# An eleventh place in the weight ring, one norm step for both tiles, and expert loops written out

## The reference

```
def reference(x, ...):
    h = x
    h = h + token_mixer(rmsnorm(h, norm_mix_w), w_in, ..., w_branch, w_out)
    h = h + moe_ffn(rmsnorm(h, norm_ffn_w), w_router, b_router, w_mlp1, b_mlp1, w_mlp2, b_mlp2)
    return rmsnorm(h, norm_final_w)

def moe_ffn(xn, ...):                       # 32 experts, top 4 of them for each token
    ...
    hdn = xb @ w_mlp1[e] + b_mlp1[e]        # 1024 -> 2048
    glu = minimum(hdn[:, :1024], 7); lin = clip(hdn[:, 1024:], -7, 7)
    act = glu * sigmoid(1.702 * glu) * (lin + 1)
    y   = act @ w_mlp2[e] + b_mlp2[e]       # 1024 -> 1024
    ...                                     # weighted sum over a token's four experts
```

## Time and profile before

| what | us |
|---|---|
| median of 3 runs (1125.34 to 1125.79) | 1125.36 |
| the profiled execution | 1125.41 |
| its span, first to last instruction | 1123.6 |
| PE busy (share of the span) | 1085.1 (97%) |
| VectorE busy | 367.8 (33%) |
| ScalarE busy | 245.6 (22%) |

### The profile page before, as it was taken

The page is one execution under the profiler, slowest core; times in us unless marked ns, Lnnn a source line. Parts: engine busy times, 40 slices in busy tenths (PEclk is TensorE's granted clock), DMA queues, the critical chain, the costliest instruction groups (busy, mean ns, idle before and its releaser), DMA issues.

```text
span 1123.6 us, 14458 instructions
## 1 busy us (share of the span) xinstructions
PE 1085.1 (97%) x5409; PEld 487.5 (43%) x5410; DVE 367.8 (33%) x813; ACT 245.6 (22%) x345; POOL 3.6 (0%) x12
## 2 busy tenths in 40 slices
PE   9999999999999999999999999999999999999996
PEld 8888888533333333333333333333333333333332
DVE  5977787422222222222222222222222222212223
ACT  4845674311111111111111111111111111111112
POOL 0000000000000000000000000000000000000000
PEclk9999999999999999999999999999999999999999
DMA  9655469999999999999999999999999999999996
GB/s 336 223 157 165 155 204 417 428 420 416 428 427 436 430 430 429 432 428 433 435 432 395 429 433 435 433 432 432 430 429 430 433 435 432 432 432 430 426 423 253
DMA packets 37877, 439.15 MB, mean 391 GB/s; under 512 B 5244, under 2 KB 5432, under 8 KB 21880
## 3 DMA queue, kind: packets, MB, share of 16 engines
q1 hardware_dynamic: 37488, 437.78, 93.3%
q10 hardware_dynamic: 360, 0.95, 0.3%
HBM read 437.67 MB, written 1.05 MB: 390 GB/s over the span
## 4 chain that ended last, share of the span: by engine, by line
PE 79%; DMA 14%; DVE 6%; issue 0%; ACT 0%; SPq 0%; DVEq 0%; PEldq 0%; ACTq 0%
PE bank L1154 33%; PE bank L1181 18%; DMA ring<-in_w_mlp_dram 11%; PE bank L798 9%; DMA late_slots<-in_w_mlp_dram 4%; PE bank L1083 3%; PE bank L1165 2%; PE bank L792 2%; PE bank L963 2%; PE bank L1011 2%; DVE xn L1670 2%; DVE xn L1667 2%; DVE xn L1674 2%; PE bank L1059 1%; PE bank L1067 1%; PE bank L1133 1%
## 5 line engine op out<-in xcount | busy, mean ns | idle before, releaser
L1154 PE MATMUL bank<-ring,xn 128*64 128x512 f32 x1232 | 276.3, 595 | 6.3 <-DMA ring<-in_w_mlp_dram 6.3
L1154 PE MATMUL bank<-late_slots,xn 128*64 128x512 f32 x880 | 197.5, 596 | 4.9 <-DMA late_slots<-in_w_mlp_dram 4.9
L1154 PEld LDWEIGHTS bank<-ring,xn 128*64 128x64 f32 x1232 | 84.4, 136 | 163.8 <-issue 150.3
L1181 PE MATMUL bank<-ring,smo 128*64 128x512 f32 x624 | 138.3, 595 | 0.0
L705 ACT ACTIVATE xn<-bank 128x512 f32<-128x512 f32 x33 | 19.7, 598 | 481.5 <-PE bank L1154 481.5
L1154 PEld LDWEIGHTS bank<-late_slots,xn 128*64 128x64 f32 x880 | 60.2, 136 | 117.9 <-issue 106.3
L1683 DVE SCALAR_TENSOR_TENSOR moe_y_lo<-bank,st,moe_y_hi 128x512 fp32r<-128x512 f32 x33 | 24.8, 750 | 235.5 <-ACT moe_y_hi L712 235.5
L1667 DVE TENSOR_SCALAR xn<-bank 128x512 f32<-128x512 f32 x33 | 22.8, 691 | 220.9 <-PE bank L1154 220.9
L1181 PE MATMUL bank<-late_slots,smo 128*64 128x512 f32 x416 | 92.1, 595 | 0.0
L1181 PEld LDWEIGHTS bank<-ring,smo 128*64 128x64 f32 x624 | 42.9, 137 | 81.1 <-issue 81.1
L712 ACT ACTIVATE moe_y_hi<-bank,st 128x512 fp32r<-128x512 f32 x33 | 22.7, 687 | 233.7 <-PE bank L1181 233.7
(11 more groups left out here) (270 smaller groups left out, 890.9 us busy)
## 6 DMA issues: line engine op xcount, KB each, us to landing
ring<-in_w_mlp_dram SPq DMA_DIRECT2D x43, 4096.0 KB, 30.4
late_slots<-in_w_mlp_dram SPq DMA_DIRECT2D x29, 4096.0 KB, 28.0
ring<-in_w_mlp_dram SPq DMA_DIRECT2D x28, 2048.0 KB, 13.4
late_slots<-in_w_mlp_dram SPq DMA_DIRECT2D x15, 2048.0 KB, 15.6
ring<-in_w_in_dram SPq DMA_DIRECT2D x22, 1024.0 KB, 5.4
late_slots<-in_w_mlp_dram SPq DMA_DIRECT2D x8, 1024.0 KB, 38.5
ring<-in_w_branch_dram SPq DMA_DIRECT2D x4, 1024.0 KB, 5.0
ring<-in_w_out_dram SPq DMA_DIRECT2D x4, 1024.0 KB, 7.1
```

Source lines behind the costliest of these rows:

```text
L1154: last = mm(B[4 + u][g * C:(g + 1) * C, :], xgT[:, k % 4, k // 4, :], by_group(held[k // 2][0][:, k % 2, u * FF:(u + 1) * FF], g), start=F ...
L1181: last = mm(B[7][g * C:(g + 1) * C, :], actT[:, j, h * C:(h + 1) * C], held[4 + h][0][:, j // 2, (j % 2) * D + g * N:(j % 2) * D + (g + 1) ...
```

## The change

- The ring has eleven places in all; `once` is gone, chunk m always goes to place m % 11, and it waits for chunk m - 11. Before, that held for chunks 11 to 15, and chunks from 16 on waited for chunk m - 10.
- 58 pairs of chunks go as one DMA of 4 MB, where 72 did: a pair that is not adjacent in SBUF (m % 11 of 3 or 9) goes as two.
- The first loads use the same semaphores and the same number of chunks behind each, with other chunk numbers.
- On PE and SP the loop over rounds is written out: every expert has its own code, with constant counts to wait for. `scatter_b2` stands ahead of expert 16.
- Of the last four chunks, the two odd ones (chunks 3 and 5 of expert 31) are cut in three pieces: 1 MB, 0.5 MB, 0.5 MB.
- The first norm: mean, root and reciprocal once for both tiles; tile 1's product on ScalarE; 12 fillers in place of 14.
- The final norm: the mean of tile 1 comes between the two halves of tile 0, and its reciprocal behind them.

```diff
-PLACES = 10
-ROUND = PLACES // 2
-QUADS = range(ROUND + 1, E - 2)
+FIRST_QUADS = 6
+PLACES = 11
+QUADS = [m for m in range(CHUNKS * FIRST_QUADS, CHUNKS * (E - 2), 2) if m % PLACES not in (3, PLACES - 2)]
...
                 if pieces == 2:
-                    for half, done in enumerate((place_landed[place], piece_landed[i])):
-                        sp.dma_start(places[place][:, half, :], src[:, half * SLOT:(half + 1) * SLOT]).then_inc(done, 16)
-                elif place is None:
-                    sp.dma_start(once[:, :, :].rearrange("p a n -> p (a n)"), src).then_inc(once_landed, 16)
+                    at = [0, SLOT, 2 * SLOT] if i % 2 == 0 else [0, SLOT, SLOT + FF, 2 * SLOT]
+                    for a, b, done in zip(at, at[1:], (place_landed[place], piece_landed[i], half_landed.get(i))):
+                        sp.dma_start(places[place].rearrange("p a n -> p (a n)")[:, a:b], src[:, a:b]).then_inc(done, 16)
...
+            for e in range(E - 1):
+                after = sp.value_load(first_item[0:1, e + 1:e + 2], min_val=1, max_val=ITEMS - 1)
+                for i in range(CHUNKS):
+                    m = CHUNKS * e + i + PLACES
+                    if m >= CHUNKS * E:
+                        continue
+                    if m not in QUADS and m - 1 not in QUADS:
                         wait_freed(after, i)
-                        load(e - c + (m + PLACES) // CHUNKS, (m + PLACES) % CHUNKS, (m - 1) % PLACES, pieces(m + PLACES))
-                    elif i % 2:
+                        load(m // CHUNKS, m % CHUNKS, m % PLACES, 2 if m >= CHUNKS * (E - 1) + 2 else 1)
+                    elif m - 1 in QUADS:
                         wait_freed(after, i)
-                        load_quad(e + 1 if i == 1 else e + 2, (i // 2 + 2) % 3, (m - 2) % PLACES)
...
             act.wait_ge(s_x, 16 * TT)
             nc.scalar.activation(xn[:, 1, :], xs[:, 1, :], ACT.Square, accum_out=st[:, 1:2]).then_inc(sumsq, 1)
             norm_root()
+            act.wait_ge(rstd, TT)
+            nc.scalar.activation(xn[:, 1, :], xs[:, 1, :], ACT.Copy, scale=st[:, 7:8]).then_inc(xn_ready, 1)
...
-            keep_warm(14, hm[:, :, :, :].rearrange("p t h d -> p (t h d)"))
+            keep_warm(12, hm[:, :, :, :].rearrange("p t h d -> p (t h d)"))
...
                     for u in range(2):
+                        if u and k == KB - 1 and 3 in in_halves:
+                            pe.wait_ge(*in_halves[3])
...
+                        if j == 3 and 4 + h in in_halves:
+                            pe.wait_ge(*in_halves[4 + h])
...
-            experts(0, chunks)
-            pe.wait_ge(opened, 2 * TT)
-            scatter_b2()
-            with pe.Fori(1, (E - 2) // ROUND) as r:
-                experts(r, lambda c: chunks_in_round(c, r))
+            for e in range(1, E - 1):
+                if e == E // 2:
+                    pe.wait_ge(opened, 2 * TT)
+                    scatter_b2()
+                first = after
+                after = pe.value_load(first_item[0:1, e + 1:e + 2], min_val=1, max_val=ITEMS - 1)
+                with pe.Fori(first, after) as i:
+                    item(i, chunks(e))
...
-            for t in range(TT):
-                norm(t)
-                v.tensor_scalar(xn[:, t, :], xs[:, t, :], st[:, 6 + t:7 + t], None, ALU.mult).then_inc(xn_ready, 1)
+            v.tensor_scalar(st[:, 2:2 + TT], st[:, 0:TT], 1.0 / D, EPS, ALU.mult, ALU.add).then_inc(meansq, TT)
+            dve.wait_ge(root, TT)
+            v.reciprocal(st[:, 6:6 + TT], st[:, 4:4 + TT]).then_inc(rstd, TT)
+            dve.wait_ge(rstd, TT)
+            v.tensor_scalar(xn[:, 0, :], xs[:, 0, :], st[:, 6:7], None, ALU.mult).then_inc(xn_ready, 1)
...
-            final_scale(0)
+            final_rstd(0)
+            final_half(0, 0)
             final_mean(1)
-            final_scale(1)
+            final_half(0, 1)
+            final_rstd(1)
+            final_half(1, 0)
+            final_half(1, 1)
```

More of the change, by code:

```diff
@@ L115, in landings @@
     for m in range(CHUNKS * E):
[L116 to L121, removed]
+        place = m % PLACES
+        if m - 1 in QUADS:
             table.append(table[-1])
@@ L200, in build @@
         pair = [ring[:, at:at + 2, :] for at in range(0, RING, 2)]
[L201 to L206, removed]
+        late_pair = [late[:, 2 * i:2 * i + 2, :] for i in range(5)]
+        places = late_pair[1:5] + pair + late_pair[0:1]
+        quads = {n: late[:, at:at + 4, :] for n, at in ((PLACES - 1, 0), (0, 2), (1, 4), (2, 6))}
+        quads.update({4 + n: ring[:, 2 * n:2 * n + 4, :] for n in range(5)})
+        assert sgm_at == sga_at + 4 * SLOT and sga_at + 4 * 2 * SLOT >= late_at + 4 * 10 * SLOT
+        wfin = places[(CHUNKS * (E - 2) + 2) % PLACES][:, 0, 0:D]
         wgh = nc.alloc_sbuf_tensor_at("w_gate_hi", [P, KB, P], F32R, offset=sgm_at)
@@ L418, in _ @@
             sp.wait_ge(slots_used, Q_OUT + 2)
-            load(1, 0, 5)
-            load(1, 2, 7)
+            first_load(1)
+            first_load(6)
             sp.wait_ge(slots_used, Q_MOE)
-            load(1, 1, 6)
-            load(1, 3, 8)
-            load(1, 4, 9)
+            first_load(2)
+            first_load(7)
+            first_load(10)
             sp.wait_ge(firsts, 1)
[L427 to L439, removed]
-                for i in range(chunks):
-                    m = CHUNKS * c + i
-                    if not (whole_second if i < 2 else whole):
+            for e in range(E - 1):
[5 more added lines that the diff above has]
+                    if m not in QUADS and m - 1 not in QUADS:
@@ L451, in _ @@
[L451 to L456 removed]
+                        load_quad(m // CHUNKS, m % CHUNKS // 2, (m - 1) % PLACES)
             after = sp.value_load(first_item[0:1, E - 1:E], min_val=1, max_val=ITEMS - 1)
[L458 removed]
+            wait_freed(after, 3)
@@ L1219, in _ @@
             v = nc.vector
-            def norm(t):
-                n = t + 1
-                dve.wait_ge(sumsq, TT)
-                v.tensor_scalar(st[:, 2 + t:3 + t], st[:, t:t + 1], 1.0 / D, EPS, ALU.mult, ALU.add).then_inc(meansq, 1)
-                dve.wait_ge(root, n)
-                v.reciprocal(st[:, 6 + t:7 + t], st[:, 4 + t:5 + t]).then_inc(rstd, 1)
-                dve.wait_ge(rstd, n)
             v.memset(hm[:, 0, 0:2, :], 0.0).then_inc(zeros, 1)
@@ L1696, in final_scale, with final_half @@
                 dve.wait_ge(rstd, 2 * TT + t + 1)
-                for n in range(2):
-                    cut = slice(n * N, (n + 1) * N)
-                    v.scalar_tensor_tensor(out=xn[:, t, cut], in0=B[2 * t + n][:, :], scalar=st[:, 6 + t:7 + t],
-                                           in1=wfin[:, cut], op0=ALU.mult, op1=ALU.mult).then_inc(normed, 1)
+            def final_half(t, n):
+                cut = slice(n * N, (n + 1) * N)
+                v.scalar_tensor_tensor(out=xn[:, t, cut], in0=B[2 * t + n][:, :], scalar=st[:, 6 + t:7 + t],
+                                       in1=wfin[:, cut], op0=ALU.mult, op1=ALU.mult).then_inc(normed, 1)
             dve.wait_ge(s_small2, 16)
```

88 lines of the change are left out of this document (32 added, 56 removed).

## The result

| | median us | runs | ratio to before, 95% interval |
|---|---|---|---|
| before | 1125.36 (1124.67 to 1128.31) | 11 | |
| the changed kernel | 1127.54 (1126.02 to 1131.29) | 11 | 1.0026 [1.0016, 1.0037] |

The change makes the kernel slower by 0.26%, 2.9 us of 1125.4. The forecast was 1124.1 with a range up to 1127.3, so the result lies outside it and on the other side. The profiled execution took 1127.33 us (span 1125.5), 1.92 more than that of before. *Written out* means that a loop's body stands in the program once for each pass.

A forecast was written before the change was run, and what follows sets the result against it. PE was taken to bound the mixer, DMA everything from about 170 us on. Terms -0.9 - 1.2 + 1.1 + 0.9 - 0.95 - 0.3 = -1.35 on the profiled 1125.41 us gave 1124.1, range 1121.3 to 1127.3.

The forecast's parts named there:

- Code written out: PE's loop copies: 22 more instruction packets cost +3.3 us, less 2.4 for two late landings avoided; sum +0.9, ends -2.4 and +24.
- the half at the end: Part of the -2.4: before's landing at 1100.97 took 60.1 us where 58.7 was due; the change should avoid this.
- The half at 275 us: Part of the -2.4: a packet on level engines made a landing 1.2 us late; the change should avoid this.
- Rival A: Instruction packets hide, spread over all 16 engines or falling into gaps: 1122.2 us, or 1120.7 with no cost; 23%.
- Rival B: Packets hit few engines, nothing levels them, lag adds up: sum +2.0 us with four engines, +8.6 with two; 10%.
- Eleventh place: In the ring: chunks from 16 on issued one chunk earlier, filling the rate dip at 240 to 260 us; -1.2 us.
- Last expert: At the end: 0.5 MB pieces let half of eight records run before chunk 3's last piece lands; -0.95 us.
- final norm: At the tail: tile 1's mean behind one half, so its root comes earlier and the last halves start sooner; -0.3 us.
- First norm: At the start: two fewer fillers and earlier norm let PE's first product start at 11.6 instead of 12.48; -0.9 us.
- Fewer pairs: In the weight stream: 14 pairs go as 28 slightly slower DMAs of 2 MB, plus the third pieces; +1.1 us.
- `scatter_b2`, 0: On PE: the same work moved to a place where PE has lead costs nothing; 2 us if the lead were gone.

The follow-up runs named there:

- written-out kernel: The kernel before with only the loops over rounds on PE and SP written out; 1128.95 us, ratio 1.0029.
- all but the place: The kernel before with everything of the change except the eleventh place in the ring (ten places, 72 DMAs of 4 MB); 1128.44 us, ratio 1.0019.
- norm and tail: The kernel before with the new first norm, third pieces and new final norm order, loops and ten places as before; 1123.1 us, ratio 0.9981.
- filler products: The changed kernel with two unused products on PE ahead of the waits for chunks 0 and 2 of experts 24 to 29; 1127.63 us, again 1127.47.
- smaller late DMAs: The changed kernel with all chunks of experts 27 to 31 in DMAs of 2 MB or less; 1127.1 us, ratio 1.0015.
- three rounds written: The kernel before with experts 16 to 30 written out on PE only, SP as before; 1130.28 us, ratio 1.0043, 5 runs.
- tail alone: The kernel before with only the last expert's third pieces and the new order of the final norm; 1124.2 us, ratio 0.9985.
- fillers and late pairs: The changed kernel with both the unused products on PE and no DMA of 4 MB from expert 27 on; 1128.53 us, ratio 1.0024.

## Why the prediction was wrong

- **Code written out, +0.9: the step that failed.** The prediction took 22/8 x 1.2 = +3.3 for the packets and set -2.4 against it, because before "paid for a packet on level engines twice where after should not". Alone, the edit costs +3.3 [+2.1, +4.4]. That this is the forecast's first half is luck, since both halves were off. The packets cost more: the landings lose 4.0 us to 17 packets in the written-out kernel, 2.9 to 16 in all but the place, 0.18 to 0.24 a packet where 0.15 was taken. Of the -2.4, the half at the end came (1.4 of slack for 1.2): at the landing of 1100.97 before's last engine went from 0.5 to 1.6 us behind the mean, and in the written-out kernel that landing brought nothing new. The half at 275 us had been read from one execution: from the eleventh chunk's landing to that of chunks 66 and 67, norm and tail gained 1.1 on before with before's loops, the written-out kernel 1.2. The rotation over eight engines is borne out, by the table above and by the durations of the packets, which repeat with period eight from 629.9 us on (1.087, 1.018, 1.018, 1.074, 1.069, 1.060, 1.099, 1.099 us, then 1.086, 1.018, 1.018, 1.073, 1.069 ...).
- **Rival A** (packets hide) is refuted. The rule of the Trainium skill ("Runtime: NRT & Kernel Launch", section "Instruction fetch mechanics") that the crossing of a block is mostly hidden holds here for PE: the item stays 26.77 us. It does not hold for the DMA engines that carry 430 GB/s of weights beside it.
- **Rival B** named what happens to the engines: with eleven places nothing levels them at 600 us, and the lag of the first 500 us is kept. It was given 10%, with engines hit four or two at a time; it was eight in turn. As a price it is not borne out: behind 613 us lag adds up with ten places too, and the landings lose as much there.
- **Eleventh place, -1.2.** The dip at 240 to 260 went as read, and chunks 66 and 67 landed 2.45 us earlier (503.98 for 506.43); 0.7 of it is the start, and norm and tail, with ten places, had them 1.36 earlier. At chunk 89 1.16 were left. "The landing was not late, so nothing is won there" was right for 600 us. Against the kernel without the place nothing is left (1.0026 against 1.0019).
- **TensorE's clock** was in no term. The prediction read PE's waits only as slack, and asked neither how long PE would stand nor what the clock does then: 1.5 us in the chain, 1.1 to 1.4 by the ratios, with the doubt told above.
- **Last expert, -0.95, and final norm, -0.3.** Alone they give -1.7 [-2.7, -0.7], so size and sign stand. In the changed kernel the piece gave nothing, because the end was by then bound by PE from the landing of chunks 176 and 177 on. The prediction did not ask how far behind that bound stood: 1.4 us.
- **First norm, -0.9.** In the trace -0.82 at the first product; by the runs -0.7, not told from 0, but 1.5 to 1.7 group against group. In the changed kernel PE waits 0.23 for ScalarE, which the prediction had covered with 0.4: the product took 1.15, not 1.06, and started later.
- **Fewer pairs, +1.1.** 430 instead of 432 GB/s from 640 to 980 us fits: 340 x 2/432 = 1.6 for pairs and packets, of which 13 packets of 1.1 us over 16 engines are 0.9. It was not tried alone. **`scatter_b2`, 0:** it shows in no wait.
- **What adds up.** Written out +3.3, norm and tail -2.1 make +1.2 for the kernel without the place; measured +2.1 [1.1, 3.2]. The sum lies inside, at the edge.

In the changed kernel's own profile, 1.92 over that of before, the terms come out like this, by landings:

| term | forecast | profile |
|---|---|---|
| start, at the landing of the eleventh chunk | -0.9 | -0.7 |
| eleventh place, and the late packet at 275 us (to chunk 67) | -1.2 - 1.2 | -1.75 |
| packets and fewer pairs (chunk 67 to 177) | +3.3 + 1.1 | +4.8 |
| end: late packet and last pieces | -1.2 - 0.95 | -1.4 |
| TensorE's clock | none | +1.5 |
| final norm | -0.3 | -0.5 |
| sum | -1.35 | +1.95 |

So in this one execution the largest miss is the clock, and the others are 0.2 to 0.8 each. The two terms at the end draw on one wait of 1.4 us and could not both be had.

Left open: the price of the clock in a typical run, and why the filler products and the smaller late DMAs together (1.0024) gave no more than either (1.0014 to 1.0017, and 1.0015); the intervals overlap, and the profile of the two together started late.

## What to carry to other kernels

Where DMA is the bound, a landing goes by the slowest of the 16 engines. Compare landings and the MB moved at them, not the rate alone: a stream can be ahead in its sum and late in its landings, as this one was by 1.3 and 2.4 us. A dip of the rate is worth filling only if the slowest engine idles in it. Code that is fetched while weights stream was paid for on those engines here, though the engine that runs it never waited; keep the loop. And before crediting a shorter wait at the end, work out where the next bound stands behind it, and how long PE will stand elsewhere.

## What the runs showed of the hardware

- An instruction packet of 16 KB held one DMA engine 1.02 to 1.10 us, and PE's packets went to eight of the sixteen engines in turn; one packet for each of the eight went with a landing 1.4 us later. PE ran 26.8 us of items on one such packet without waiting, and the loop over five experts ran with none at all from 500 to 1090 us.
- PE's granted clock fell to 1.2 GHz for 3.41 us behind waits of 2.29 to 3.30 us in the middle of busy work, and not in before, whose waits were 1.78 at most. Such a wait did not always bring it: 2.54 us in the written-out kernel, 2.69 in all but the place and 2.56 in the changed kernel's second profile passed at 2.4 GHz.
- The clock also fell once near 41 us in five of the 14 profiles (written out, three rounds written, all but the place, tail alone, fillers and late pairs). Their first expert issue is at 158.4 to 159.9 instead of 156.7 to 157.8. The two groups of before's runs, 2.0 us apart (1125.5 and 1127.5) with a mean granted clock of 0.997 to 0.998 and 0.996, fit such a fall; only profiles show when it came.
